# Two feed-forward layers on one core: their second products taken by Strassen's seven products

## The reference

```python
# first block: sliding-window attention, retention, gated merge, then
h = rms_norm(x, norm_ffn)                                   # D_FF = 2816
x = x + (silu(h @ w_gate) * (h @ w_up)) @ w_down
x = rms_norm(x, final_norm)
# second block: dilated attention, spatial gating, then
h = rms_norm_2(x, g_pre_ffn)                                # D_FF_2 = 4096
f = square(relu(h @ w_ff1)) @ w_ff2
return x + rms_norm_2(f, g_post_ffn)
```

## Time and profile before

| what | value |
|---|---|
| median of 3 runs | 2899.72 us (2893.6 to 2900.33) |
| profiled execution, its own time | 2899.71 us |
| its span, first to last instruction | 2897.9 us |
| mean granted TensorE clock | 0.975 of full |
| PE busy | 2785.0 us, 96% |
| VectorE / GpSimd / ScalarE busy | 1349.2 / 995.2 / 842.6 us |
| moved by DMA | 248.28 MB, mean 86 GB/s |

### The profile page before, as it was taken

How to read it: one execution, slowest core, us unless ns; L and a number is a source line. 1 busy time by engine, 2 the same in 40 slices (tenths; PEclk the granted TensorE clock), 3 DMA queues, 4 the chain that set the end, 5 groups by cost and what they waited for, 6 DMA issues and landing times.

```text
span 2897.9 us, 34574 instructions
## 1 busy us (share of the span) xinstructions
PE 2785.0 (96%) x13622; PEld 2330.2 (80%) x13622; DVE 1349.2 (47%) x2385; ACT 842.6 (29%) x1584; POOL 995.2 (34%) x746
## 2 busy tenths in 40 slices
PE   7999999999999999999999899999996999999998
PEld 6767888777887888888788678989876888878887
DVE  4352111251233644444556621157627666656666
ACT  4352111122222423323121511057624233321121
POOL 2121100243233456555623432235244434322221
PEclk9899999999999999999999999989998999999999
DMA  4101220101341122222522122122023333333223
GB/s 164 49 34 45 90 71 32 62 15 48 107 170 66 67 87 79 81 88 99 214 88 95 67 75 67 40 63 60 19 96 99 99 115 111 134 141 108 96 88 102
DMA packets 104175, 248.28 MB, mean 86 GB/s; under 512 B 17829, under 2 KB 36901, under 8 KB 103845
## 3 DMA queue, kind: packets, MB, share of 16 engines
q1 hardware_dynamic: 104014, 246.07, 25.6%
HBM read 192.18 MB, written 53.59 MB: 85 GB/s over the span
## 4 chain that ended last, share of the span: by engine, by line
PE 85%; DVE 6%; POOL 3%; ACT 2%; issue 2%; DMA 1%; SPq 0%; POOLq 0%; DVEq 0%; ACTq 0%
PE PS L658 8%; PE PS L660 8%; PE PS L661 8%; PE PS L455 7%; PE PS L456 7%; PE PS L457 7%; PE PS L681 6%; PE PS L682 6%; PE PS L683 6%; PE PS L775 3%; PE PS L471 3%; PE PS L473 3%; PE PS L472 3%; PE PS L752 1%; PE PS L540 1%
## 5 line engine op out<-in xcount | busy, mean ns | idle before, releaser
L1781 POOL TENSOR_TENSOR WL<-WRAW,WH 128x1024 fp32r<-128x1024 f32 (+1 forms) x154 | 296.9, 1930 | 1063.2 <-ACT WH L828 1063.1
L828 ACT ACTIVATE WH<-WRAW 128x1024 fp32r<-128x1024 f32 (+1 forms) x262 | 223.6, 865 | 463.5 <-PE PS L683 374.8
L681 PE MATMUL PS<-WH,H1L 128*128 128x512 f32 x800 | 314.0, 393 | 9.9 <-DVE X L1554 9.6
L682 PE MATMUL PS<-WL,H1H 128*128 128x512 f32 x800 | 313.0, 391 | 0.0
L683 PE MATMUL PS<-WH,H1H 128*128 128x512 f32 x800 | 313.0, 391 | 0.0
L1556 DVE TENSOR_TENSOR X<-PS,X 128x512 f32<-128x512 f32 x368 | 242.6, 684 | 144.7 <-PE PS L683 138.4
L455 PE MATMUL PS<-HH,WL 128*128 128x512 f32 x736 | 294.2, 400 | 2.0 <-DVE HL L1268 1.9
L456 PE MATMUL PS<-HL,WH 128*128 128x512 f32 x736 | 291.3, 396 | 0.0
L457 PE MATMUL PS<-HH,WH 128*128 128x512 f32 x736 | 290.5, 395 | 0.0
L658 PE MATMUL PS<-HH,WL 128*128 128x512 f32 (+1 forms) x672 | 251.0, 373 | 8.0 <-DVE HS L1506 4.3
L660 PE MATMUL PS<-HL,WH 128*128 128x512 f32 (+1 forms) x672 | 249.4, 371 | 0.0
(11 more groups left out here) (336 smaller groups left out, 5527.7 us busy)
## 6 DMA issues: line engine op xcount, KB each, us to landing
WRAW<-in_u_f SPq DMA_DIRECT2D x64, 512.0 KB, 3.5
WRAW<-in_u_in SPq DMA_DIRECT2D x50, 512.0 KB, 3.5
HRAW<-scr_h SPq DMA_DIRECT2D x25, 1024.0 KB, 6.0
scr_h<-HS SPq DMA_DIRECT2D x96, 256.0 KB, 2.2
WRAW<-in_u_gu SPq DMA_DIRECT2D x44, 512.0 KB, 3.4
scr_x<-X SPq DMA_DIRECT2D x24, 512.0 KB, 3.0
WRAW<-in_u_dn SPq DMA_DIRECT2D x22, 512.0 KB, 3.5
X<-in_x SPq DMA_DIRECT2D x16, 512.0 KB, 8.4
```

What stands on the lines that cost most here:

```text
L681: e.matmul(PS[:, b, :], hl, wh, start=(t == ks[0] and f == 0), stop=False)
L682: e.matmul(PS[:, b, :], hh, wl, start=False, stop=False)
L1781: e.tensor_tensor(lo, raw, hi.bitcast(F32), ALU.subtract).then_inc(*c.inc("w_lo_p", i))
```

## The change

The second product of each layer is taken by the same seven products. The hidden pairs are cut into chunks: 6 and 5 pairs in layer 1, 8 and 8 in layer 2. A chunk is a product of a 1024 x (256 g) matrix by a (256 g) x 1024 one, g being its number of pairs. Its quarters A11 to A22 are 512 rows by g hidden tiles (each pair gives one tile to the left half and one to the right), and B11 to B22 are the quarters of the weights. In order the seven steps are P1 = A11 B11, P2 = A12 B21, P5 = S1 T1, P6 = S2 T2, P7 = S3 T3, P3 = S4 B22, P4 = A22 T4.

- **TensorE.** A step accumulates its g tiles in four banks, item by item: one item is four row tiles by three matmuls. The last step of the layer goes bank by bank.
- **Operands of A.** SyncE loads quarters (`load_quarter`) into `HHF`/`HLF` in runs of 2 KB, for chunk 0 during the last block of the first product. VectorE forms the sums S1 to S4 in place (`d_sum`), two steps ahead. ScalarE and VectorE split them into a ring of 8 slots, one step ahead (`d_split`). VectorE now makes all low parts, of A and of the weights.
- **Operands of B.** The sums T1 to T4 of all 27 pairs are formed once, by GpSimd, in the projections of the first attention (24 pairs) and in `q2` (3 pairs): SyncE loads 1 MB, GpSimd does four subtractions of 128 x 512, SyncE stores 1 MB to the new `scr_t`. Two buffers take turns. In the feed-forward layer half units of two tiles are fetched into `WRAW`.
- **Results.** ScalarE copies P1 to the new buffer `DV`; VectorE adds P6 and P7 into it and adds P2, P5 (twice), P3 and P4 to `X`; GpSimd adds `DV` to four quarters of `X`. In layer 1 `X` is first loaded with the residual (4 MB), in place of the eight adds of GpSimd.
- **Ends.** P3 ends row tiles 0 to 3 together, P4 ends tiles 4 to 7. The norm of layer 1 has its small sums rearranged. The norm of layer 2 has GpSimd multiply by the gain (`XG`) while ScalarE squares, and VectorE scale and add the residual in one instruction; the residual is loaded in two transfers.
- The transfers of the decay tables (`DECT`, `DECQ`) move from before `rq` to after `rv`'s seventh bank of the second half.

```diff
@@ TensorE
+        def ffn_down(lay):
+            for n, (k, p) in enumerate(STEPS[lay]):
+                g = len(CHUNKS[lay][k])
+                def part(i, b):
+                    key, op = d_key(lay, n, b), DOP[lay, n, i]
+                    if i == 0:
+                        open_bank(key)
+                    w.wait_ge(*c.at("d_al", (lay, n, i)))
+                    w.wait_ge(*lo_done(op))
+                    ...
+                    e.matmul(dst, hl, wh, start=(i == 0), stop=False)
+                    e.matmul(dst, hh, wl, start=False, stop=False)
+                    mm = e.matmul(dst, hh, wh, start=False, stop=(i == g - 1))
+                    ...
+        ffn_down(1)
+        for tt in range(4):
+            back(3, tt)
@@ ScalarE
+        def d_split(lay, n, items):
+            for i in items:
+                ...
+                w.wait_ge(*d_source(lay, k, a_kind, i))
+                e.activation(d_slot(lay, n, i, 0), d_tile(a_kind, i), ACT.Copy).then_inc(*c.inc("d_ah", (lay, n, i)))
+                w.wait_ge(*half_read(ops[op][2] - NHS))
+                w.wait_ge(*c.at(f"raw{ops[op][1] % NRAW}", ops[op][1]))
+                e.activation(half_slot(WH, op), d_weights(lay, n, i), ACT.Copy).then_inc(*c.inc("w_hi", op))
@@ VectorE
+            for n in range(last - 1):
+                for i in range(8):
+                    if n + 2 < last and DPROD[STEPS[lay][n + 2][1]][0][0] == "S" and i < len(CHUNKS[lay][STEPS[lay][n + 2][0]]):
+                        d_sum(lay, n + 2, i)
+                    if i < 4 and n and STEPS[lay][n - 1][1] != "P1":
+                        add(n - 1, i)
+                    if i < len(CHUNKS[lay][STEPS[lay][n + 1][0]]):
+                        d_split(lay, n + 1, [i])
+            for tt in range(N_FIN):
+                if tt < NT:
+                    add(last - 2 + tt // 4, tt % 4)
+                fin(tt)
@@ GpSimd
+        def down_sums(key):
+            ...
+            w.wait_ge(*c.at(f"ts{t_set(g)}", ("in", g)))
+            e.tensor_tensor(b12, b12, b11, ALU.subtract).then_inc(*c.inc("t_d", (g, "T1")))
+            w.wait_ge(*c.at("t_d", (g, "T1")))
+            e.tensor_tensor(b22, b22, b12, ALU.subtract).then_inc(*c.inc("t_d", (g, "T2")))
+            w.wait_ge(*c.at("t_d", (g, "T2")))
+            e.tensor_tensor(b11, b22, b11, ALU.subtract).then_inc(*c.inc("t_d", (g, "T3")))
+            e.tensor_tensor(b21, b21, b22, ALU.subtract).then_inc(*c.inc("t_d", (g, "T4")))
+                for b in range(0 if k == 0 and lay == 2 else 4):
+                    add_v("11", "P1", b)
+                for b in range(4):
+                    add_v("12", "P6", b)
+                for b in range(4):
+                    add_v("21", "P7", b)
+                ...   # then "22", "P7"
@@ SyncE, last block of the first product
+                    if (m, c0, wd) == BLOCKS[lay][-1]:
+                        for kind, half in FIRST_IN.get(p, ()):
+                            w.wait_ge(*bk.full(key))
+                            load_quarter(lay, 0, kind, half)
+                        while p == "P7" and n_fetch[0] <= DUNIT[lay, 0, 2]:
+                            fetch()
@@ the last norm
+            e.tensor_tensor(XG[:, tt % 2, :], X[:, tt, :], NG[:, 0, :], ALU.mult).then_inc(*c.inc("n_f", (6, tt)))
             rsqrt(6, tt, VV[1][:, tt:tt + 1], RR[1][:, tt:tt + 1])
+            e.scalar_tensor_tensor(out=X[:, tt, :], in0=XG[:, tt % 2, :], scalar=RR[1][:, tt:tt + 1],
+                                   in1=NX[tt // 6][:, tt % 6, :], op0=ALU.mult, op1=ALU.add).then_inc(*c.inc("n_out", tt))
```

More of the change, by code:

```diff
@@ L337, in ready @@
     def ready(i, key):
-        return all(p < NHS or bk.order.get(LAST.get(p - NHS), 1 << 30) <= bk.order[key] for p in places(i))
+        return ops[i][0] != "d" and all(p < NHS or bk.order.get(LAST.get(p - NHS), 1 << 30) <= bk.order[key] for p in places(i))
     def b_tile(kind, n):
@@ L349, in raw_users @@
             return [OPU[n]], None
+        if order[n][0] == "d":
+            return [i for i, op in enumerate(ops) if op[0] == "d" and op[1] == n], None
         first = next(i for i, (kind, m, pos) in enumerate(ops) if kind == "B11" and m in (n, n - 1))
@@ L703, in pe_program @@
                 proj_t(("zu", j, half), U["u_in2", j], half, HH, HL)
-                if half == 0 and j < 3:
-                    back(3, 5 + j)
+            if half == 0:
+                for tt in range(4, NT):
+                    back(3, tt)
         for tt in range(NT):
@@ L1079, in ffn_down @@
                 fin(tt)
-                for nh in range(2):
-                    feed(("dl", lay, tt, nh))
+                if tt == 4:
+                    feed(d_key(lay, last - 2, 3))
+            feed(d_key(lay, last - 1, 3))
         def square_g(tt):
@@ L1234, in fin2 @@
         def fin2(tt):
-            w.wait_ge(*bk.out(("dl", 2, tt, 0)))
-            w.wait_ge(*bk.out(("dl", 2, tt, 1)))
+            if tt >= NT:
+                return
+            for done in row_done(2, tt):
+                w.wait_ge(*done)
             if tt >= 1:
@@ L1799, in feed @@
         def feed(key):
-            while n_split[0] < len(ops) and ready(n_split[0], key):
+            while n_split[0] < len(ops) and (ops[n_split[0]][0] == "d" or ready(n_split[0], key)):
                 i = n_split[0]
@@ new lines, in ffn_down, with fin1 @@
+            for s in range(9 if lay == 1 else 0, N_FIN):
+                fin(s)
+            feed(d_key(lay, last - 1, 3))
+        def fin1(s):
+            if s - 3 in ROW_AT:
+                tt = ROW_AT[s - 3]
+                rsqrt(31, tt, RQ[:, 24 + tt:25 + tt], RQ[:, 32 + tt:33 + tt])
+            if s in ROW_AT:
+                tt = ROW_AT[s]
+                w.wait_ge(*c.at("gb0", 3))
+                w.wait_ge(*c.at("n_sq", (3, tt)))
+                e.tensor_tensor(X[:, tt, :], X[:, tt, :], NG[:, 0, :], ALU.mult).then_inc(*c.inc("n_f", (3, tt)))
+            if s - 1 in ROW_AT:
+                tt = ROW_AT[s - 1]
+                rsqrt(3, tt, RQ[:, tt:tt + 1], RQ[:, 8 + tt:9 + tt])
@@ L2089, in fetchable @@
+            e.dma_start(WRAW[:, n % NRAW, 0:512 * g].rearrange("p (g c) -> p g c", g=g), src).then_inc(
+                *c.inc(f"raw{n % NRAW}", n, 16))
         def fetchable(n, key):
-            return n < NRAW or all(ready(i, key) for i in RAW_USERS[n - NRAW][0])
+            return n < NRAW or all(ready(i, key) or ops[i][0] == "d" for i in RAW_USERS[n - NRAW][0])
         def feed(key):
-            while n_fetch[0] < len(order) and fetchable(n_fetch[0], key):
+            while n_fetch[0] < len(order) and order[n_fetch[0]][0] != "d" and fetchable(n_fetch[0], key):
@@ L2280, in sync_program @@
                 feed(("q2", j, half))
+                down_tiles(("q2", j, half))
         def load_g(h):
```

683 lines of the change are left out of this document (419 added, 264 removed).

## The result

The changed kernel takes **2821.2 us**, the median of 4 runs (2815.44 to 2825.28), against 2899.14 us of the kernel before (4 runs, 2893.6 to 2900.33): ratio **0.9733**, 95% interval 0.9709 to 0.9758. The forecast was 2830, in the range 2810 to 2862. The profiled execution took 2817.68 us by its own time (span 2815.6, mean clock 0.978), 82.0 less than the profiled one of before.

A forecast was written before the change was run, and what follows sets the result against it. TensorE's number of matmuls was taken to bound the kernel (busy 96% of the span). Terms -73.5 + 4 - 10 + 1 + 8.4 + 0 = -70.1 us, from 2899.7, gave 2830 us, range 2810 to 2862.

The forecast's parts named there:

- matmuls: Second products: 2268 matmuls for 2592, 324 fewer at 0.2267 us each, all on the path: -73.5 us.
- VectorE's pace: Second products: TensorE stays the bound, narrowly in layer 1's second chunk; GpSimd's adds slow VectorE: +4 us (0 to 20).
- entries: Starts of both second products: copies into X no longer hold TensorE, transfer stalls replace them: net -10 us (-16 to 0).
- between the layers: Layer 1's second product to zu: four rows end together, 16.9 us lost against 15.8 before: +1 us (-8 to +12).
- kernel's end: Last matmul to last result: four rows at 4.15 us each under shared ports, 14.9 us open against 6.5: +8.4 us.
- sums T: Projections: 140 us of GpSimd work and 54 MB more moved, with TensorE never waiting: 0 us (0 to +10).
- 92 of 95: Chunk of 5 pairs: VectorE's counted time, including 21 us for GpSimd's adds, against TensorE's time, in us.
- the lead of three items: Second products' steps: the ring of 8 slots lets VectorE work three items ahead and take up the densest step's excess.
- Rival (1): GpSimd's adds and VectorE's low parts hold each other in every dense step: +16 us, 2846 us; chance 0.14.
- rival (4): VectorE can't work ahead, each low part waiting for ScalarE's 0.62 us first: +164 us, 2990 us; chance 0.04.
- Rival (2): Transfers set entries and chunk changes: 10 us more at entries, 10 at the two changes, 2850 us; chance 0.12.
- zu starts near +29, that is 15.4 after P4: Between layer 1 and zu: the row norms' chain, timed from P3's end; of the 15.4 us, 4.2 are transposes, 11.2 idle.

The follow-up runs named there:

- P7 twice: Changed kernel with TensorE running each of layer 2's two P7 steps twice into the same banks, 192 matmuls more: 2863.97 us, ratio 0.9891.
- end on VectorE: Changed kernel with layer 2's last norm scaled by gain and power on VectorE, GpSimd only taking the powers: 2811.3 us, ratio 0.9711.
- the sums alone: Kernel before, with the sums T formed, loaded and stored but read by nobody, and the decay tables' load moved: 2896.82 us, ratio 0.9988.
- the idle one: Kernel before, with TensorE made to wait for the last row of x2 before zu, no work added: 2906.19 us, ratio 1.0018.
- low parts twice: Changed kernel with VectorE making each low part of A twice, 189 subtractions of 128x512 more: 2865.22 us, ratio 0.9889.

## Why the prediction was right, and where it was not

| term | forecast | measured | by what |
|---|---|---|---|
| matmuls | -73.5 | -73.5 | 2268 for 2592; P7 twice |
| VectorE's pace | +4 | 0 | 0.4 us lost in layer 1's product |
| entries | -10 | -10.5 | -7.6 layer 1, -2.9 layer 2 |
| between the layers | +1 | +8.7 | lost 24.5 after, 15.8 before |
| kernel's end | +8.4 | +7.6 | timeline, end on VectorE |
| sums T | 0 | 0 | the sums alone |
| unchanged stages | none | -14.6 | half clock in other places |
| sum | -70.1 | -82.3 | profiled: -82.0, the rest is rounding |

**Matmuls.** Right, and the reason is shown from the other side: 192 matmuls put back cost 43.4 us.

**VectorE's pace.** That TensorE stays the bound was right, and so was that the ports cost VectorE time, but their price was too high. In the changed kernel what VectorE's 128x512 instructions last beyond 0.70 us adds up to 27.5 us in layer 1's product and 22.6 in layer 2's, for 28 operations of GpSimd on `DV` each: 1.0 and 0.8 us apiece for my 1.29, 50 us for my four times 21. The busy shares of 82% in layer 2 and 90% in layer 1's first chunk look like the 124 of 152 and 103 of 114 us that I counted, but partly by luck: an instruction that isn't queued is recorded with 0.68 us, not 0.60. Layer 1's second chunk, 83% for my 92 of 95, has more room. The choice of +4 was too careful: as long as a step isn't much over TensorE's time, the lead of three items takes all of it. Rival (1) and rival (4) fell with it: the subtractions last 0.68 to 1.02 us on average and TensorE doesn't wait inside the steps.

**Entries.** The size held, and in layer 2 the mechanism too. It loses 5.3 us where I took 4: the late wait for VectorE's low part behind a late fetch, and the half clock after it. Moving the last add ahead of the low parts took both away. Layer 1 loses 0.4 where I took 2. Rival (2) fell: DMA was busy 0.80 in that entry without a wait.

**Between the layers.** The step that failed: "zu starts near +29, that is 15.4 after P4". It was 23.8. I had counted one split of weights on GpSimd ahead of the rows. The trace has more in their chain. That split starts 2.0 us after P3's end (1573.16 for 1571.13), since ScalarE's copy ahead of it waits for a weight transfer until 1572.02; most of that wait of 7.7 us lies before P3's end and costs nothing. This accounts for some 2 of the 8.4 missing us, by the timeline alone, as no run took it away. And from 1591.4 on, in the middle of the rows, three copies of weights on ScalarE (2.94 us) stand, with a subtraction of 2.6 on VectorE and a split of 2.5 on GpSimd. Moving these behind the rows gave 6.6 to 7.0 in the gap. Half of it or more came back in `zu`, as longer waits for rows and as half clock, which counting the gap alone did not see. The count of what each moved `feed` issues was missing for ScalarE, though the prediction did it for GpSimd.

**The kernel's end.** Right in size (14.9 forecast, 14.1 measured) and cause: without GpSimd's multiplication it was 7.2. The parts of a row, 2.39, 0.55 and 1.28, make 4.22 and not the 4.15 of the forecast; measured are 4.08. The Trainium skill ("SBUF — State Buffer", "Who interferes with whom") gives the two engines' shared port as an exclusive lock; the timeline above agrees, with 3.36 us for an instruction of 1.28.

**Unchanged stages.** I gave them no term. 4.9 of the 14.6 are chance. 9.7 are one stretch at half clock of 24 us or more that came in all three profiles of the kernel before and its sums variant, in the idle one, and in 2 of 10 of the changed kind. That the change makes it rarer fits these counts, and the untraced executions too. By their mean clocks, the 50 of the kernel before that ran beside the experiments have 146 us at half clock on average, the nine of the changed kernel 128, although the changed one has more of it in its gap and at its end, where TensorE is mostly idle. The stretch isn't bound to the kernel either, as executions of 2882 and 2884 us of the kernel before, at a mean clock of 0.981, must have had less half clock too. But the cause isn't shown: the idle gap, the one cause tried, is excluded as sufficient.

Without these 14.6 us the terms come to -67.7, 2.4 less than the forecast's -70.1. That this is so near is in part luck: I took 4 too much for VectorE's pace and 0.5 and 0.8 too much at the entries and the end, and 7.7 too little between the layers. So the profiled execution beat the forecast by 12 us, and the median by 9, for a reason that no step of mine had, while my steps together promised 2.4 too much.

## What to carry to other kernels

Where TensorE has 96% of the span, the count of matmuls prices a change to within a few us, and all that remains is at the seams: list there every instruction that each engine issues between the last matmul and the next, the weight splits of the next stage included. An operation that GpSimd takes over from VectorE "beside" it can lengthen a serial chain, since the two lengthen each other; at the end of this kernel one engine with more instructions was 6.9 us faster. And where VectorE's queue never runs empty, a GpSimd operation can stand for 25 us. And add up single edits by the stages that they touch, not by medians: here stages of unchanged code moved by 10 us between executions, and the medians promised 18.8 where 14.1 came.

## What the runs showed of the hardware

- VectorE was busy 94 to 96% of windows of 100 to 300 us (286.83 of 300 us with the low parts made twice). Queued instructions of 128x512 start 0.60 us apart there, with two inputs in SBUF or one in PSUM; a recorded duration is 0.68.
- A GpSimd add of 128x512 with two inputs in SBUF took 1.29 us alone. While four of them ran one behind another, VectorE's subtractions beside them took 1.78 and 1.83 us for 0.68 (changed kernel, 1504 to 1508 us). When VectorE had its own queued without a pause, one such add lasted 25.7 us and another, in layer 1, 20.5, while VectorE kept its 0.60 (low parts twice).
- GpSimd's power of one column took 0.55 us alone and 1.46 to 1.48 beside VectorE's add of 128x1024: the lengthening goes both ways, also for an instruction of one column.
- The granted clock at one place of the program takes one of two courses between executions, and the stage took 827 us by one and 837 to 841 by the other. Where it fell, in six profiles of fourteen, it began at the same place of the program within 1 us. What decides it is open.
